# The second layer's modulation vector inside the first expert layer: products and sums on VectorE instead of products on POOL and sums on ScalarE

## What is computed, cut to what matters

```
for i in range(2):                                   # two layers of the first block
    mod_l = split(silu(c)     @ w_mod[i] + b_mod[i], 6)   # six vectors of 1024
    mod_c = split(silu(c_ctx) @ w_mod[i] + b_mod[i], 6)
    nl = modulate(rmsnorm(hl, norm1_g[i]), mod_l[0], mod_l[1])
    nc = modulate(rmsnorm(hc, norm1_g[i]), mod_c[0], mod_c[1])
    ... mixer, residual ...
    ff = peer(concat(nc, nl), peer_w_q[i], peer_subkeys[i], peer_u[i], peer_v[i])   # "expert layer"
    ... residual ...

def peer(h, w_q, subkeys, u, v):      # 16384 experts, 8 heads, 16 experts of each head are used
    q = h @ w_q;  s = q @ subkeys (two halves);  top 16 of each half;  top 16 of their 256 sums
    act = gelu(h @ u[idx]);  return sum(g * act * v[idx])
```

## Time and profile before

| | us |
|---|---|
| median of three runs | 4586.32 |
| their lowest and highest | 4578.13, 4597.22 |
| the profiled execution | 4580.37 |
| its span in the profile | 4578.7 |
| PE, DVE, ACT, POOL busy | 4122.4, 3232.1, 2223.1, 487.6 |

### The profile page before, as it was taken

One profiled execution on the slowest core, in us unless ns is written; L12 is line 12 of the kernel. 1 busy time (PEld: TensorE's weight loads), 2 busy tenths in 40 slices (PEclk: granted clock), 3 DMA queues, 4 the chain that ended last, 5 costly groups with the idle time before them and its releaser, 6 DMA issues. The chain is left out here.

```text
span 4578.7 us, 69836 instructions
## 1 busy us (share of the span) xinstructions
PE 4122.4 (90%) x24777; PEld 3642.5 (80%) x24777; DVE 3232.1 (71%) x7162; ACT 2223.1 (49%) x4342; POOL 487.6 (11%) x365
## 2 busy tenths in 40 slices
PE   7787879999999999889999999699888999998898
PEld 2646778999977777669999777598876889887687
DVE  6355998999878887458877576565486556548655
ACT  6234553367633333335578455354355444445543
POOL 0001662422322221000000000000000000000000
PEclk9898999999999999999999999899998999999999
DMA  7103668888999997227777888554443445444343
GB/s 274 46 17 125 223 197 281 286 278 302 342 358 337 341 341 256 90 90 215 212 235 246 268 261 260 170 189 155 129 136 131 177 158 188 159 130 132 133 179 138
DMA packets 393734, 937.20 MB, mean 205 GB/s; under 512 B 37228, under 2 KB 211564, under 8 KB 376796
## 3 DMA queue, kind: packets, MB, share of 16 engines
q1 hardware_dynamic: 356576, 799.21, 52.7%
q0 software_dynamic: 36864, 134.23, 8.4%
HBM read 839.92 MB, written 93.39 MB: 204 GB/s over the span
## 5 line engine op out<-in xcount | busy, mean ns | idle before, releaser
L173 DVE TENSOR_TENSOR w_low__5<-w_raw,w_high__5 128x512 fp32r<-128x512 f32 x576 | 454.7, 814 | 63.1 <-ACT w_high__5 L168 63.1
L161 PE MATMUL hidden<-hT_high__2,w_high__5 128*128 128x384 f32 (+1 forms) x1280 | 434.5, 339 | 64.8 <-DVE w_low__5 L173 63.9
L168 ACT ACTIVATE w_high__5<-w_raw 128x512 fp32r<-128x512 f32 x576 | 339.9, 624 | 249.2 <-DMA w_raw<-in_peer_u 118.9
L173 DVE TENSOR_TENSOR w_low__6<-w_raw__2,w_high__6 128x512 fp32r<-128x512 f32 x544 | 362.6, 689 | 118.3 <-ACT w_high__6 L168 103.6
L162 PE MATMUL hidden<-hT_low__2,w_high__5 128*128 128x384 f32 (+1 forms) x1280 | 426.1, 333 | 0.0
L163 PE MATMUL hidden<-hT_high__2,w_low__5 128*128 128x384 f32 (+1 forms) x1280 | 425.8, 333 | 0.0
L168 ACT ACTIVATE w_high__6<-w_raw__2 128x512 fp32r<-128x512 f32 x544 | 321.8, 624 | 71.2 <-DMA w_raw__2<-in_peer_v 32.8
L161 PE MATMUL hidden__3<-hT_high__4,w_high__6 128*128 128x256 f32 x1152 | 332.5, 289 | 0.5 <-DVE hT_low__4 L275 0.4
L162 PE MATMUL hidden__3<-hT_low__4,w_high__6 128*128 128x256 f32 x1152 | 327.3, 284 | 0.0
L163 PE MATMUL hidden__3<-hT_high__4,w_low__6 128*128 128x256 f32 x1152 | 326.9, 284 | 0.0
L161 PEld LDWEIGHTS hidden<-hT_high__2,w_high__5 128*128 128x128 f32 x1280 | 247.9, 194 | 75.4 <-issue 48.7
(11 more groups left out here) (976 smaller groups left out, 12481.5 us busy)
## 6 DMA issues: line engine op xcount, KB each, us to landing
w_raw<-in_peer_u SPq DMA_DIRECT2D x128, 512.0 KB, 5.5
w_raw<-in_peer_v SPq DMA_DIRECT2D x128, 512.0 KB, 5.7
w_raw__2<-in_peer_u SPq DMA_DIRECT2D x128, 512.0 KB, 4.4
w_raw__2<-in_peer_v SPq DMA_DIRECT2D x128, 512.0 KB, 4.9
w_ring<-in_w_mod SPq DMA_DIRECT2D x96, 256.0 KB, 4.4
gathered_rows<-in_w_mod_tiles SPq DMA_DIRECT2D x48, 512.0 KB, 4.5
activated_dram<-activated SPq DMA_DIRECT2D x128, 192.0 KB, 6.7
routing_dram<-routing SPq DMA_DIRECT2D x24, 1024.0 KB, 9.6
```

The costliest lines, as they stand in the source:

```text
L161: nc.tensor.matmul(out, lhs[0], rhs[0], start=start, stop=False, skip_group_check=True)
L168: return nc.scalar.activation(high, src, ACT.Copy)
L173: return nc.vector.tensor_tensor(low, src, high.bitcast(F32), ALU.subtract)
```

## The change

POOL's products and ACT's sums go. In their place DVE issues one `tensor_tensor_reduce` for each of the 64 products, which multiplies and writes the sum, at the end of its slot m + 1 (at most 48), behind the low halves and the ranking step. Each waits for the one before (`summed`) and for its tile. SP's load of tile m now waits for the last sum of tile m - 3 (`summed`) where it waited for POOL's product (`multiplied`).

```
@@ class Modulation, sp_load
         if m >= r:
-            sp.wait_ge(self.multiplied, self.last_of[m - r] + 1)
+            sp.wait_ge(self.summed, self.last_of[m - r] + 1)
         sp.dma_start(self.ring[:, m % r, :], self.w[self.order[m]]).then_inc(self.loaded[m % r], 16)

-    def pool_multiply(self, pool, n):
-        m, _, v = self.work[n]
+    def dve_product(self, dve, n):
+        m, t, v = self.work[n]
         r = self.ring.shape[1]
         if n == 0:
-            pool.wait_ge(self.silu_loaded, 32)
-        pool.wait_ge(self.loaded[m % r], 16 * (m // r + 1))
-        if n >= 2:
-            pool.wait_ge(self.summed, n - 1)
-        self.nc.gpsimd.tensor_tensor(self.products[:, n % 2, :], self.ring[:, m % r, :], self.silu_rows[v], ALU.mult) \
-            .then_inc(self.multiplied, 1)
-
-    def act_sum(self, act, n):
-        _, t, v = self.work[n]
-        act.wait_ge(self.multiplied, n + 1)
-        product = self.products[:, n % 2, :]
-        self.nc.scalar.activation(product, product, ACT.Copy, accum_out=self.columns[:, t, v:v + 1]) \
+            dve.wait_ge(self.silu_loaded, 32)
+        else:
+            dve.wait_ge(self.summed, n)
+        dve.wait_ge(self.loaded[m % r], 16 * (m // r + 1))
+        self.nc.vector.tensor_tensor_reduce(self.products[:, 0, :], self.ring[:, m % r, :], self.silu_rows[v], 1.0, 0.0,
+                                            ALU.mult, ALU.add, accum_out=self.columns[:, t, v:v + 1]) \
             .then_inc(self.summed, 1)
@@ experts, gpsimd
-                for n in range(mod.n):
-                    mod.pool_multiply(pool, n)
                 pool.wait_ge(mod.summed, mod.n)
@@ experts, scalar, end of each slot
-                for n in range(mod.n if items else 0):
-                    if mod_sum_at[n] == s:
-                        mod.act_sum(act, n)
@@ experts, vector, behind the ranking step of each slot
+                for n in range(mod.n if items else 0):
+                    if mod_sum_at[n] == s:
+                        mod.dve_product(dve, n)
```

More of the change, by code:

```diff
@@ L949, in __init__ @@
         self.silu_loaded = st.sem("silu_rows_loaded")
-        (self.bias_loaded, self.multiplied, self.summed, self.ready, self.stored) = (
-            st.sem(x) for x in ("b_mod_loaded", "mod_multiplied", "mod_summed", "mod_ready", "mod_rows_stored"))
+        (self.bias_loaded, self.summed, self.ready, self.stored) = (
+            st.sem(x) for x in ("b_mod_loaded", "mod_summed", "mod_ready", "mod_rows_stored"))
     def sp_load(self, sp, m):
```

## The result

The changed kernel takes 4597.49 us (median of 20 runs), the kernel before 4585.29 beside it: 1.0028 times, 95% interval 1.0016 to 1.0039. That is 12 us slower, where 11 were forecast; the interval is 7 to 18 us. The profiled execution has a span of 4596.5 us against 4578.7. A few executions of some kernels took hundreds of us longer at another granted clock; the ratios leave them out, and the medians given here are at most 2 us higher by them.

A forecast was written before the change was run, and what follows sets the result against it. DVE was taken to bound the stream up to slot 46. -91 + 72.3 + 35 - 4.3 (earlier waits replaced) - 1.2 = +11 us against the median 4586.3 gave 4597 us, with 8 in 10 from 4568 to 4621.

The forecast's parts named there:

- DVE set the pace: Stream up to slot 46: DVE, busy 99.5 of 100 us and 104.9 of 105, bounds it.
- What goes, -91: DVE's standing beside POOL's products ends: 88 us in the stage and 2.9 us ahead of it.
- What is added, +72: DVE up to slot 46: 62 products at 1.14 us, plus 1.6 us for waits on a preceding sum.
- At slots 46 to 48: Around the exponential: ACT's sum goes and two products lie in DVE's waits or behind `chosen_experts`, -1.2 us.
- SP's queue, +35: Weights' pieces, asked for behind the tile's wait for DVE's sum, come late and make DVE wait 35 us.
- The way of 5.4 us: From the product's end through tile issue and weights' landing to DVE's low half: 5.3 to 5.4 us without store.
- the second rival: Each slot's two transfers hurt each other, landing 5.5 us instead of 4.5: +35 in all, 4621 us; chance 0.20.
- The sum: All terms together: +11 us at the time when the experts are chosen, 4597 us for the kernel.
- PE's clock: PE's granted clock, 0.93 before: nothing put on it, as PE's gaps only change place.
- The hidden wait: Rival: loads asked for a slot later still land in time, so -20 us, 4566 us; chance 0.11.
- The low halves' other cause: Rival: low halves stay slow for another cause than POOL, nothing recovered, +99 us, 4685 us; chance 0.02.
- The rule against the change: With DVE saturated, moving work to ScalarE or GpSimd may make sense; set aside for the shared-lock rule, no size given.

The follow-up runs named there:

- 64 more products: Kernel with the weights' piece asked for ahead of the modulation tile, each of the 64 products made twice: 4636.7 us, 1.0103 of the kernel before.
- with none: Changed kernel without the modulation's loads and products, sums set to zero: 4510.56 us, 0.9841 of the kernel before.
- the unused ones: Weights asked for ahead of the tile, plus 64 POOL products nobody uses, one released by each of DVE's sums: 4704.12 us, 1.0257 of the kernel before.
- both mends: Changed kernel with the weights' piece asked for ahead of the tile and a ring of four modulation tiles: 4560.9 us, 0.9945 of the kernel before.
- the queue mended: Changed kernel with either the weights' piece asked for ahead of the tile (4565.89 us) or four modulation tiles instead of three (4565.33 us).
- a fourth tile: Changed kernel with a ring of four modulation tiles instead of three, order of requests kept: 4565.33 us, 0.9949 of the kernel before.
- twenty products on POOL: Weights asked for ahead of the tile, 20 of 64 products back on POOL, released behind both low halves: 4549.75 us, 0.9927 of the kernel before.
- the release at the ranking step: Weights asked for ahead of the tile, plus 20 unused POOL products released when both low halves are done: 4566.23 us, 0.9945 of the kernel before.
- the release at the low halves: Weights asked for ahead of the tile, plus 20 unused POOL products released by the previous slot's last sum: 4610.69 us, 1.0051 of the kernel before.
- the release on the low half: Weights asked for ahead of the tile, 20 real products on POOL released after the slot's first low half: 4546.06 us, 0.9924 of the kernel before.

## Why the prediction was right, point by point

**DVE set the pace.** Right. With 64 more products at 1.26 us, 74 of 81 us arrive at the gather, and with none PE takes over as the bound.

**What goes, -91.** Right in kind and near in size. Low halves 686 ns for the 684 taken, comparisons 2284 for 2284, copies 170 for 220. Ahead of the stage the column chunk takes 3.68 us (424.52 to 428.20) where 7.1 less 2.9 was expected: the low half in it, added as 0.6 us, lies in DVE's wait for ACT. That POOL's products were the cause is shown from one side by the changed kernel, which keeps the tiles' loads, and from the other by the unused ones.

**What is added, +72.** Right: 1.14 us from start to start and 1.26 where the second waits for the first (441.30 to 442.56), for the 1.24 taken. At slots 46 to 48 the prediction charged both products of slot 46 and took 1.2 us off. In the traces the stretch from `centre` to `chosen_experts` takes 12.2 us before (691.42 to 703.61) and 12.0 after (708.21 to 720.17), with three products in it: they took the place of 3.6 us of waits for ACT.

**SP's queue, +35.** Right, and the term that decides the sign. The way of 5.4 us came out to 0.1. The waits add up to 42.1 in 436 to 704 and 39.9 from slot 3 on, instead of 35; 35 above those of before (6.9) were forecast as 31. The worked list had 3.1, 0, 1.8, 1.2, 1.8, 0, 3.1, 0.5 us for slots 3 to 10; the trace has 2.9, 0.5, 1.2, 1.8, 1.3, 0.3, 4.7, 0. The 4.7 at slot 9 stands for 3.1 in the working. SP's queue and ACT there, changed kernel:

```profile
469.09 0.43 SPq L1222 DMA_DIRECT2D w_raw<-in_peer_u  x1
471.43 0.33 SPq L961 DMA_DIRECT2D gathered_rows<-in_w_mod_tiles  x1
471.81 0.43 SPq L1222 DMA_DIRECT2D w_raw<-in_peer_u  x1
...
475.39 1.15 ACT L168 ACTIVATE w_high__5<-w_raw 128x512 fp32r<-128x512 f32 x2 [2.15 <-DMA w_raw<-in_peer_u]
```

The piece asked for at 469.09 is taken up 6.3 us later, the one of 471.81 6.1 us later (477.87), and ACT waits for both. Slot 8 was short, so the next tile and piece were asked for 2.3 and 2.7 us behind the first, which fits the second rival's mechanism in small. But 587.07 was asked for as close behind another and taken up after 4.9 us, so why these two were so long is not settled. And PE would have held up slot 9 in any case: with both mends its low half waits 6.1 us.

**The sum.** +11 forecast at the gather, +15.4 in the traces, and +12 in the medians. The 4 us more are in the main the waits, 35 for 31. That the median lies within 1 us of the 4597 forecast is luck, since the interval spans 11 us and the single terms are off by 1 to 5. PE's clock, put at nothing, was granted at 0.91 over the stage before and 0.87 after, with PE busy 230.0 and 237.6 us; ACT waits for PE 19 us before (436 to 700) and 5 after (436 to 715), so PE was not what held the stage up more. Behind the gather the two kernels are alike: 3873.9 us to the end of the span before, 3874.6 after. So the shift reached the end, as the prediction had it.

**The rivals.** The hidden wait (4566) is what the kernel would be with the queue mended, and that is where those kernels came out, at 4565.9 and 4565.3. Of the pieces that ACT waited for in 440 to 704, that of 444.20 is taken up after 4.3 us and later ones mostly after 4.2 to 5.2 (485.75 to 490.58, 492.28 to 497.44). Five take 6.0 to 6.5: the two above and those of 514.66, 610.17 and 626.72. So the second rival's landings exist, as a minority. With the pair of transfers unchanged and a fourth tile the waits went, so it fell as the main effect. The low halves' other cause fell with the changed kernel itself, where they take 686 ns.

**The rule against the change** (the Trainium skill, page "Perfetto Trace Analysis", section "Optimizing Scalar/DVE Operations"), that moving work off a saturated VectorE to ScalarE or GpSimd may make sense, was set aside in the prediction. The runs give it its due: with twenty products on POOL the kernel gains 22 us in the stage, with 64 unplaced ones it loses. The same section warns that, since the two share a port, it might not help; here it depended on which instruction stood beside the product.

What stays open: the kernel before has a cost of 1.4 us for each POOL product on average, the mix of those that meet low halves and those that don't; it was not taken apart product by product. Which instructions of one input a POOL product holds up was not tested one by one. And why five of the transfers took over 6 us is not settled.

## What to carry to other kernels

When work moves from one engine to another, ask what waits for its end: here the queue's head waited for it, and an unrelated load stood behind; asking for that load first, or one more buffer, was worth 0.7% and the sign of the change. A bound engine that waits nowhere may still be standing: compare the same instruction's mean time in two stretches. And if two engines hold each other up, as POOL and DVE do here, place the one's work beside those of the other's instructions that don't lengthen, rather than moving all of it.

## What the runs showed of the hardware

- A POOL product (fp32, 128 x 1024, two inputs) takes 2.37 to 2.42 us beside DVE's ranking steps (the release at the ranking step). Released while the first of two low halves of DVE (two inputs in SBUF) runs, it takes 2.75 to 2.80 us; the first low half is not touched and the second stands until it is over: 3.4 us for a pair that takes 1.2 (the release at the low halves). Released while the second runs, with MAX8 behind it, POOL's product takes 2.76 to 2.80 and DVE loses nothing (the release on the low half). This agrees with the Trainium skill, page "SBUF — State Buffer", section "Who interferes with whom": the shared port pair is an exclusive lock, and the order of issue decides who is blocked.
- MAX8, FIND_INDEX8 and MATCH_REPLACE8 (0.27 to 0.29 us) are not lengthened by more than 0.01 us in the mean by a POOL product beside them. Twenty products beside ranking steps of these and of reductions cost 0.9 us in all. A CAST of 128 x 512 took 1.88 us for 0.43, and copies of 128 x 32 took 992 ns for 220, beside POOL's products in the kernel before.
- 512 KB asked for right behind another 512 KB on the same queue lands after 4.2 us, 4.8 with a store behind it, in the kernel before; in the changed one it is taken up after 4.3 and 4.8. Where four such transfers were asked for within 3.1 us (468.72 to 471.81, changed kernel), two were taken up after 6.1 to 6.3; the same spacing gave 4.9 elsewhere (587.07).
